# Layer 1's normalised rows turned and shifted one tile at a time, in layer 0's sum of rows

## What is computed

```python
for i in range(DEPTH):
    ...
    h_lat = rmsnorm(x, g_mix[i]) * (1 + sc1) + sh1
    h_ctx = rmsnorm(xc, g_mix[i]) * (1 + csc1) + csh1
    y_lat, y_ctx = token_mixers(h_lat, h_ctx, not last, ...)
    x = x + gt1 * y_lat
    ...
    f_out = moe_ffn(jnp.concatenate([f_lat, f_ctx], axis=0), *moe_args)
    x = x + gt2 * f_out[:B * S].reshape(B, S, D)
    xc = xc + cgt2 * f_out[B * S:].reshape(B, C, D)
return rmsnorm(x, g_final)
```

## Time and profile before

| | |
|---|---|
| median of 3 runs | 3370.18 us (3364.9 to 3371.2) |
| the profiled execution, its own time | 3383.25 us |
| span of the profiled execution | 3381.4 us |
| mean granted TensorE clock | 0.984 |
| busy: TensorE, VectorE, ScalarE | 94%, 52%, 40% |
| mean DMA rate | 215 GB/s |
| sum of rows of layer 0, first load issued to last add ended | 1858.67 to 1927.00 us |
| last add ended to first projection of layer 1 | 1927.00 to 1940.10 us |

### The profile page before, as it was taken

How to read it: one execution, slowest core, us unless ns; L and a number is a source line. 1 busy time by engine, 2 the same in 40 slices (tenths; PEclk the granted TensorE clock), 3 DMA queues, 4 the chain that set the end, 5 groups by cost and what they waited for, 6 DMA issues and landing times.

```text
span 3381.4 us, 47597 instructions
## 1 busy us (share of the span) xinstructions
PE 3181.1 (94%) x14840; PEld 2225.7 (66%) x14840; DVE 1745.9 (52%) x2409; ACT 1336.9 (40%) x1883; POOL 594.1 (18%) x751
## 2 busy tenths in 40 slices
PE   6999999999998999999999699999998899999996
PEld 3457967899654766667676346876764576666662
DVE  1344252133265766676675525342425677676665
ACT  2244152212123555555554225342212455555551
POOL 0000310000043222222232000020004222233220
PEclk9989999999999999999999899999999999999999
DMA  6410212333515999999997910102240999999986
GB/s 220 126 63 7 78 32 76 131 131 131 202 40 203 370 377 362 361 372 385 377 376 265 373 52 1 54 20 89 88 151 29 344 374 356 351 365 358 345 318 250
DMA packets 224802, 727.19 MB, mean 215 GB/s; under 512 B 55890, under 2 KB 104660, under 8 KB 165396
## 3 DMA queue, kind: packets, MB, share of 16 engines
q1 hardware_dynamic: 179508, 633.37, 51.2%
q0 software_dynamic: 45184, 92.28, 7.3%
HBM read 707.64 MB, written 84.24 MB: 234 GB/s over the span
## 4 chain that ended last, share of the span: by engine, by line
PE 66%; DMA 19%; DVE 5%; issue 4%; ACT 3%; SPq 1%; another core or an unknown queue 1%; DVEq 0%; POOLq 0%; POOL 0%; ACTq 0%
PE ps L835 11%; PE ps L837 10%; PE ps L836 10%; PE ps L828 7%; DMA region_v<-in_w_exp_up 7%; PE ps L916 6%; PE ps L857 5%; PE ps L1025 5%; DMA ring<-in_w_exp_up 4%; PE ps L1127 4%; DMA region_k<-in_w_exp_up 4%; PE ps L1048 3%; DMA ring<-y_rows 2%; PE ps L944 1%; ACT region_h_split L1205 1%
## 5 line engine op out<-in xcount | busy, mean ns | idle before, releaser
L857 PEld LDWEIGHTS ps<-con,region_c 128*128 128x128 f32 x1878 | 249.1, 169 | 129.3 <-issue 96.5
L857 PE MATMUL ps<-con,region_c 128*128 128x128 f32 x1878 | 279.1, 278 | 23.2 <-DVE region_c L1818 10.5
L1983 POOL DMA_INDIRECT y_rows<-region_q,idx_out x141 | 142.4, 1010 | 896.0 <-DVE region_q L1587 805.1
L837 PE MATMUL ps<-region_x_split,ring_split 128*128 128x384 f32 (+2 forms) x800 | 282.8, 354 | 0.0
L835 PE MATMUL ps<-ring_split,region_q_split 128*128 128x512 f32 x568 | 227.8, 401 | 13.2 <-DVE ring_split L1554 12.9
L835 PE MATMUL ps<-region_h_split,region_q_split 128*128 128x512 f32 x560 | 224.4, 401 | 12.1 <-DVE ring_split L1554 11.3
L1205 ACT ACTIVATE region_q<-ps 128x512 f32<-128x512 f32 (+1 forms) x145 | 87.6, 604 | 359.8 <-PE ps L916 313.5
L837 PE MATMUL ps<-ring_split 128*128 128x512 f32 x568 | 222.5, 392 | 0.0
L837 PE MATMUL ps<-region_h_split,ring_split 128*128 128x512 f32 x560 | 219.4, 392 | 0.0
L1382 ACT ACTIVATE region_c<-ps 128x768 f32<-128x768 f32 (+1 forms) x48 | 33.8, 705 | 412.2 <-PE ps L837 412.2
L1205 ACT ACTIVATE region_c<-ps 128x512 f32<-128x512 f32 (+3 forms) x129 | 84.8, 657 | 225.6 <-PE ps L857 125.2
(11 more groups left out here) (312 smaller groups left out, 6915.6 us busy)
## 6 DMA issues: line engine op xcount, KB each, us to landing
ring<-in_w_mod SPq DMA_DIRECT2D x24, 2048.0 KB, 8.1
region_k<-in_w_exp_gate SPq DMA_DIRECT2D x48, 1024.0 KB
region_k<-in_w_exp_up SPq DMA_DIRECT2D x48, 1024.0 KB
region_k<-in_w_exp_down SPq DMA_DIRECT2D x48, 1024.0 KB
ring<-in_w_exp_gate SPq DMA_DIRECT2D x47, 1024.0 KB
ring<-in_w_exp_up SPq DMA_DIRECT2D x47, 1024.0 KB
ring<-in_w_exp_down SPq DMA_DIRECT2D x47, 1024.0 KB
region_v<-in_w_exp_gate SPq DMA_DIRECT2D x46, 1024.0 KB
```

The source lines that it names most:

```text
L837: last = mm(o, wl, xh, start=False, stop=k == len(stationary) - 1)
L857: last = nc.tensor.transpose(ps[0:t.shape[1], at:at + t.shape[0]], t, ident[0:t.shape[0], 0:t.shape[0]])
L1983: pool.indirect_dma_start(Y8, bass.IndirectOffsetOnAxis(ap=idx_out[:, s:s + 1], axis=0), yb[:, s, :], None, bounds_check=TOK * TOPK - 1, o ...
```

## The change

In the list of jobs, layer 1 loses its eight "h" jobs. The turning goes into layer 0's sum of rows instead. On TensorE, `turn_next(l, i - 1)` follows the sum of tile i, and `turn_next(l, 5)` the loop: it waits for the normalised tile and for the eviction of the tile before, and turns 8 blocks of 128x128 into slot 2, which the sum of rows doesn't use. On ScalarE, the loop over tiles now first evicts the tile before (8 instructions of 128 columns with scale and shift, into `hT`), then squares, takes the root and writes the normalised row; the normalised rows have two buffers instead of six, `XN_next` in region_q. Of the last tile ScalarE evicts four blocks and VectorE the other four. The "ckv", "cq" and "kr" jobs of layer 1 wait for that one semaphore. Since `hT` is now written during the sum of rows, `half_b`'s third buffer moves out of region_h into two pieces of the experts' memory in region_q and region_c. Beside this the two semaphores of the shared expert's weights become one, so that "sg" and "sd" both wait for all three transfers.

```diff
--- before.py
+++ after.py
@@ -168,7 +168,7 @@
     for l in range(DEPTH):
         A = active(l)
 
-        for k in range(DK):
+        for k in range(DK if l == 0 else 0):
             add("h", l, k, drain=alt[k % 2])
         for c in range(2):
             add("ckv", l, c, drain="act", panel=("ckv", l))
@@ -427,7 +427,8 @@
             return w[:, 0:4096].rearrange("p (g k n) -> p g k n", g=2, k=DK)
         wdn = [w[:, 4096:6144].rearrange("p (c n) -> p c n", c=2) for w in WSL]
         half_a = [ring[:, 4096 * i:4096 * i + 4096] for i in range(3)]
-        half_b = [w[:, 0:4096] for w in (K, VY, HT)]
+        half_b = [[K[:, 0:2048], K[:, 2048:4096]], [VY[:, 0:2048], VY[:, 2048:4096]], [Q[:, 2048:4096], C[:, 0:2048]]]
+        XN_next = Q[:, 0:2048].rearrange("p (a d) -> p a d", a=2)
 
 
         PS = stack.enter_context(nc.psum_tensor("ps", [P, 4096], F32))
@@ -452,6 +453,7 @@
         rms_rec, rms_sqrt, cn_ready = sem("rms_rec"), sem("rms_sqrt"), sem("cn_ready")
         roped, rope_copied = sem("roped"), sem("rope_copied")
         max_ready, exp_ready, o_full, o_drained = sem("max_ready"), sem("exp_ready"), sem("o_full"), sem("o_drained")
+        h_turned, h_evicted = sem("h_turned"), sem("h_evicted")
         rd_ready = sem("rd_ready")
         sink_sum, sink_exp = sem("sink_sum"), sem("sink_exp")
         h_high, h_low, w_high, w_low = sem("h_high"), sem("h_low"), sem("w_high"), sem("w_low")
@@ -460,7 +462,7 @@
         kk_ready, kk_zero, u_zero, pooled = sem("kk_ready"), sem("kk_zero"), sem("u_zero"), sem("pooled")
         f_ready, s_h = sem("f_ready"), [sem("s_h0"), sem("s_h1")]
         w_ready, s_w = sem("w_ready"), [sem("s_w0"), sem("s_w1")]
-        sh_silu, s_sgu, s_sd = sem("sh_silu"), sem("s_sgu"), sem("s_sd")
+        sh_silu, s_shared = sem("sh_silu"), sem("s_shared")
         setup_dve, tab_ready = sem("setup_dve"), sem("tab_ready")
         s_turns = sem("s_turns")
         cT_zero = sem("cT_zero")
@@ -729,8 +731,8 @@
                 load_until(("router", l))
                 for g, w in enumerate((w_sh_gate, w_sh_up)):
                     sp.dma_start(w_sgu[:, 2048 * g:2048 * g + 2048].rearrange("p (k n) -> p k n", k=DK), kpn(w[l], 0, DE))\
-                        .then_inc(s_sgu, 16)
-                sp.dma_start(w_sd.rearrange("p (k n) -> p k n", k=2), kpn(w_sh_down[l], 0, D)).then_inc(s_sd, 16)
+                        .then_inc(s_shared, 16)
+                sp.dma_start(w_sd.rearrange("p (k n) -> p k n", k=2), kpn(w_sh_down[l], 0, D)).then_inc(s_shared, 16)
 
                 sl = L[l]
 
@@ -794,7 +796,7 @@
                         sp.wait_ge(combined, before + i - 2)
                     for q in range(2):
                         at = 2 * D * q
-                        sp.dma_start(half_b[i % 3][:, at:at + 2 * D], y[:, 4096 + at:4096 + at + 2 * D]).then_inc(s_part_b[i][q], 16)
+                        sp.dma_start(half_b[i % 3][q], y[:, 4096 + at:4096 + at + 2 * D]).then_inc(s_part_b[i][q], 16)
                         sp.dma_start(half_a[i % 3][:, at:at + 2 * D], y[:, at:at + 2 * D]).then_inc(s_part_a[i][q], 16)
                     if i >= 3:
                         save(i - 3)
@@ -864,6 +866,13 @@
                 pe.wait_ge(L[l][f"gat{s}"], gathered)
                 v = xg[s][:, 0:D].rearrange("s (p k) -> s k p", k=DK)
                 turn(ps, [(k * P, v[:, k, :]) for k in range(DK)]).then_inc(L[l]["tr_done"], 1)
+
+            def turn_next(l, t):
+
+                pe.wait_ge(xn_ready, NT * (l + 1) + t + 1)
+                if t:
+                    pe.wait_ge(h_evicted, t)
+                turn(slot[2], [(k * P, XN_next[:, t % 2, k * P:k * P + P]) for k in range(DK)]).then_inc(h_turned, 1)
 
             def moe(l, last_fills):
 
@@ -964,8 +973,11 @@
                     col += P * a[1] if len(a) > 1 else 0
                     w = chunks(panel((key, l)), DK, width)
                     rows = ROPE if kind == "kr" else P
-                    after(pe, "h", l, DK - 2)
-                    after(pe, "h", l, DK - 1)
+                    if l == 0:
+                        after(pe, "h", l, DK - 2)
+                        after(pe, "h", l, DK - 1)
+                    else:
+                        pe.wait_ge(h_evicted, NT + 1)
                     last = project(ps, [w[:, k, col:col + rows] for k in range(DK)], [hT[:, k, :] for k in range(DK)],
                                    full(l, kind), rows)
                 elif kind in ("rq", "rk"):
@@ -1139,7 +1151,7 @@
                         last = mm(ps[:, 0:E], hT[:, k, t * P:t * P + P], w[:, k, :], start=k == 0, stop=k == DK - 1)
                 elif kind == "sg":
                     l, t = a
-                    pe.wait_ge(s_sgu, 32 * (l + 1))
+                    pe.wait_ge(s_shared, 48 * (l + 1))
                     w = w_sgu.rearrange("p (g k n) -> p g k n", g=2, k=DK)
                     after(pe, "f", l, t)
                     for k in range(DK):
@@ -1151,7 +1163,7 @@
                     last = turn(ps, [(cc * P, hb[:, n % 2, cc * P:cc * P + P]) for cc in range(2)])
                 elif kind == "sd":
                     l, t = a
-                    pe.wait_ge(s_sd, 16 * (l + 1))
+                    pe.wait_ge(s_shared, 48 * (l + 1))
                     w = chunks(w_sd, 2, D)
                     n = active(l).index(t)
                     after(pe, "sT", l, t)
@@ -1189,10 +1201,14 @@
                             if j % 2 == 0:
                                 pe.wait_ge(s_part_b[i][j // 2], 16 * (l + 1))
                             for half in range(2):
-                                at = D * j + 512 * half
-                                last = mm(slot[i % 2][:, 512 * half:512 * half + 512], ident, half_b[i % 3][:, at:at + 512],
+                                at = D * (j % 2) + 512 * half
+                                last = mm(slot[i % 2][:, 512 * half:512 * half + 512], ident, half_b[i % 3][j // 2][:, at:at + 512],
                                           start=j == 0, stop=j == TOPK // 2 - 1)
                         last.then_inc(b_summed, 1)
+                        if l < DEPTH - 1 and i:
+                            turn_next(l, i - 1)
+                    if l < DEPTH - 1:
+                        turn_next(l, NT - 1)
                 if job.drain:
                     last.then_inc(filled, 1)
 
@@ -1416,18 +1432,26 @@
 
                         def normed(t):
                             act.wait_ge(pre_rstd, NT * l + t + 1)
-                            copy_scaled(XN[:, t, :], XT[:, t, :], rstd[:, t:t + 1]).then_inc(xn_ready, 1)
-
+                            copy_scaled(XN_next[:, t % 2, :], XT[:, t, :], rstd[:, t:t + 1]).then_inc(xn_ready, 1)
+
+                        def evict(t, ks):
+                            act.wait_ge(h_turned, t + 1)
+                            s = 0 if t >= CT else 1
+                            for k in ks:
+                                ins = A_(hT[:, k, t * P:t * P + P], slot[2][:, k * P:k * P + P], ACT.Identity,
+                                         scale=column(l + 1, "A1", s, k), bias=column(l + 1, "sh1", s, k))
+                            ins.then_inc(h_evicted, 1)
+
+                        act.wait_ge(setup_dve, 2 * l + 3)
                         for t in range(NT):
+                            if t:
+                                evict(t - 1, range(DK))
                             act.wait_ge(combined, t + 1)
                             A_(junk, XT[:, t, :], ACT.Square, accum_out=ssq[:, t:t + 1]).then_inc(pre_ssq, 1)
                             act.wait_ge(pre_var, NT * l + t + 1)
                             A_(rstd[:, t:t + 1], ssq[:, t:t + 1], ACT.Sqrt).then_inc(pre_rstd, 1)
-                            if t < 4:
-                                normed(t)
-                        act.wait_ge(combined, NT)
-                        for t in range(4, NT):
                             normed(t)
+                        evict(NT - 1, range(DK // 2))
                     else:
                         for i, t in enumerate(active(l)):
                             act.wait_ge(combined, NT + i + 1)
@@ -1622,6 +1646,12 @@
                     if i:
                         finish(i - 1)
                 finish(len(A) - 1)
+                if l < DEPTH - 1:
+                    dve.wait_ge(h_turned, NT)
+                    for k in range(DK // 2, DK):
+                        ins = ts(hT[:, k, TOK - P:TOK], slot[2][:, k * P:k * P + P], column(l + 1, "A1", 0, k),
+                                 column(l + 1, "sh1", 0, k), ALU.mult, ALU.add)
+                    ins.then_inc(h_evicted, 1)
 
             vec.memset(cT[:], 0.0).then_inc(cT_zero, 1)
             dve.wait_ge(s_con, 32)
```

## The result

| | before | after |
|---|---|---|
| median of 4 runs | 3368.88 us (3364.9 to 3371.2) | 3395.43 us (3394.94 to 3397.88) |
| ratio | | 1.008, 95% interval 1.0069 to 1.0092 |
| span of the profiled execution | 3381.4 us | 3393.9 us |
| sum of rows, C(0) to C(5) | 1877.66 to 1927.00 = 49.3 us | 1872.97 to 1945.65 = 72.7 us |
| tail, C(5) to the first projection | 13.1 us | 13.2 us |

The change costs 26.55 us (3395.43 - 3368.88). The last three lines of the table hold 25.85 of it: 23.34 in the sum of rows, 0.09 in the tail, 2.42 in the projection. (The two profiled spans differ by less, 12.5 us, because the profiled execution of before was a long one: its own time, 3383.25 us, lies 14.4 above its median, while the profiled execution of the changed kernel, 3395.7, lies 0.3 above its own.

The account below looks back on a forecast made before the run. TensorE, 94% busy, bounds the kernel; DMA sets layer 0's sum of rows at 9.9 us a tile. Sum of rows +22.3, tail -0.2, projection +2.0 make +24.1 us on 3370.18: 3394.3 us, range 3380 to 3403.

Parts of the forecast that it names:

- C(0) to C(5): Layer 0's sum of rows, from the first tile's last add to the sixth's; forecast to grow by 22.3 us.
- The ring: Layer 0's sum of rows: TensorE idles 5.67 us, then turn and sum; 15.5 us in place of 9.9.
- The clock: TensorE in layer 0's sum of rows: falls to 1.2 GHz in each ring, comes back after 4.3 us.
- Rival B: Layer 0's sum of rows: clock stays up, ring 13.5 us, +14.4 us in all, 3384 us; chance 0.10.
- the turn at 1.2 GHz: TensorE, in each ring and the tail: 8 transposes at 7 a us take 1.15 us.
- The tail: From the last add's end to layer 1's first projection matmul: 12.9 us, before 13.1; gain 0.2 us.
- X(5): Tail: end of ScalarE's normalised copy of the last tile, 9.5 us after T, the last add's end.
- The projection at half rate: Layer 1's projection starts at 1.2 GHz: +2.0 us, range 0 to 3.
- Parts at nothing: Moved half-row buffer, one shared-expert semaphore, layer 1's rotated PSUM slots and modulation waits: no cost.
- Rival A: Layer 0's sum of rows: turns fit TensorE's holes; 3.5 to 4.8 us gained, 3366 us; chance 0.06.
- X(i - 1) comes behind S(i): Layer 0: normalised copy of tile i - 1 ends after TensorE's sum of tile i, first 6.7 us behind.
- Rival D: Layer 0's rings: transposes don't bring the clock back, 4.3 us count from the sum; +2.3 us, 3396.6; chance 0.07.

Follow-up runs that it names:

- e5: Changed kernel with 6 filler matmul calls on TensorE ahead of each turn's wait; ratio 1.0040 to the kernel before.
- e10: Kernel before with only the two semaphores of the shared expert's weights made one; ratio 1.0004.
- e2: Changed kernel with VectorE's finish(i - 1) of layer 0 moved ahead of its wait for TensorE's sum of tile i; ratio 0.9988 to the kernel before.
- e6: Changed kernel with VectorE's finish(i - 1) of layer 0 behind its first add of tile i, ahead of the second half's landing wait; ratio 0.9992 to before.
- e8: e7 with 6 filler matmul calls ahead of the last turn's wait alone; ratio 0.9977 to the kernel before.
- e7: e6 with layer 1's first projection weights loaded as soon as tile 3 is summed; ratio 0.9988 to the kernel before.
- e11: e8 with 8 filler calls instead of 6 ahead of the last turn and one more behind it; ratio 0.9971 to the kernel before.

## Why the prediction was right

- **The ring.** Its order (sum, adds, finish(i - 1), root, copy, turn, sum) was read off the code and the rows, and the timeline shows it. 15.5 us were forecast and 15.7 measured. The idle part was 5.58, forecast 5.67. Turn and sum took 9.9, 10.7, 9.4 and 10.4 us, mean 10.1, forecast 9.85 and, as bounds, 9.3 to 10.75. C(0) to C(5) grew by 23.3 us, forecast 22.3.
- **The clock.** Fallen in every ring, back after 3.0 to 5.6 us, mean 4.4, forecast 4.3. That it would fall within 5.67 us rested on two cases, 2.3 and 5.2 us; in one ring it took 5.1, so the margin was thin. Rival B (it stays up, +14.4 us) was wrong for this kernel, but e5 made it true by filler and found +13.5.
- **A term mis-sized: the turn at 1.2 GHz.** "7 transposes a us" gave 1.15 us for eight. It was 1.76 (1884.64 to 1886.40), 0.22 each. A window counts each record that reaches into it, at both edges, so a count of seven in one microsecond is not a rate; the spacing of starts would have been. In the ring, turn and sum share the time at 1.2 GHz, so the 0.6 us count half: 0.3 us, which is what turn and sum were short by. The two turns of the tail cost more, as the next point shows.
- **The tail.** Forecast 12.9, measured 13.2. X(5) came at T + 9.48, forecast 9.5. The eviction of 128 columns, extended from the earlier trace rows, takes 0.46 us by itself (forecast 0.445) and 0.36 in a row (0.40). That the whole came out so close is in part luck: the evictions of the two groups began 0.5 and 0.4 us later than forecast (T + 3.74 for 3.25, T + 11.54 for 11.1), and the shorter evictions and what stands between them gave most of it back. The 250 ns of the Trainium skill (VectorE: DVE Perf Modes, the TRN2 errata), which the prediction weighed, was the worse price here, as the rows at 256 columns suggested.
- **The projection at half rate.** 2.4 us, forecast 2.0.
- **Parts at nothing.** The semaphore alone: nothing (e10). The moved buffer and the rotated slots ran in e2 and e6, which are no slower than the kernel before; they weren't tried alone.
- **Rival A**, the turns in TensorE's holes, was refused for this kernel because X(i - 1) comes behind S(i). e6 moves just that point, and the rest of A came true: combines 9.9 us apart, tail near the weights' landing at T + 8.9. A's price, 3.5 to 4.8 us gained in the tail, was found too (4.2), but it left out the half-rate start of the projection (32.8 us for its 96 records, 1.5 more than before), so e6 gains only 2.7 us (0.9992) and that can hardly be told from nothing.
- **Rival D**, that transposes don't bring the clock back: against it the third ring, where the clock was back 3.0 us after a turn's start and only 1.2 us after the sum's (1918.17 to 1919.4).

The sum, +24.1 us, was 2.45 short of the measured 26.55: 1.04 of it in the sum of rows, 0.29 in the tail, 0.42 in the projection, and 0.70 outside of these stretches.

## What to carry to other kernels

When work is slipped between two steps of an in-order engine, write down for each thing it waits for where that stands in the order of the other engine: here the turn waited for a statement that stood behind an add which needed TensorE's own sum, and one statement moved up by a few lines took 27 us away. The wait on TensorE cost twice here, once as idle time and once as the clock that fell in it, and each half was about 13 us. And check that a step's release isn't put, on the releasing engine, behind a wait that has nothing to do with it.

## What had not been expected

- In e8 the clock fell to 1.2 GHz at 1924.8 with 1.1 us of turning between idle stretches of 2.02 and 1.69 us. In e2 it fell at 1896.4 (0.70 over 1896 to 1897), 0.3 us into a turn that followed a single idle stretch of 1.97 us. Yet in e7 it stayed at 1.00 from 1910 to 1913, through an idle stretch of 2.50 us. So the length of the longest hole doesn't tell by itself whether it falls; what does is open. In e11, with 0.30 and 0.83 us, it stayed up. The window of e2, and the window and the row of e7:

```profile
1896.00:1897.00 1.00, 0.90 (x6) 0.90 (x7) 1.00 (x1) 0.04 (x1) 0.00 (x0) 0.70 0.98 410
```

```profile
1910.00:1913.00 3.00, 0.85 (x2) 0.49 (x3) 1.10 (x3) 2.18 (x4) 0.00 (x0) 1.00 0.99 407
...
1912.15 3.70 PE L1207 MATMUL ps<-region_c,con 128*128 128x512 f32 x8 [2.50 <-DMA region_c<-y_rows]
```

- The wait for a turn's result: from the start of a group of 8 transposes to ScalarE's first eviction there are 2.01 us at 1.2 GHz (1955.18 to 1957.19) and 1.13 at 2.4 GHz (e5, 1892.21 to 1893.34), so in these runs the lower clock lengthened the chain through TensorE by 0.88 us though only 8 transposes were done.
